# Retention decoder step: key-value product from rounded hi and lo parts, state updates beside the output projection, state transfers on GpSimd's queue

## The chip, the cores and the metric

The kernel runs on one core of one Trainium2 chip. Its time is the device time of one execution in microseconds (us); the number given for a kernel is the median of several runs. TensorE (PE) does the matmuls, VectorE (DVE) and ScalarE (ACT) do elementwise work, GpSimd (POOL) sets constants, and SyncE (SP) issues transfers. Each engine works through its own list in order and waits on semaphores for the others.

## The reference

One step of a hybrid decoder: a prompt of 528 rows (16 learned rows and 512 tokens) and 8 samples with one new row each, model width 1024. Layer 0 is a retention mixer and a gated FFN with a causal convolution of width 3; layer 1 is a short convolution mixer and a second such FFN; a last norm follows. The change is in the retention mixer, which has 4 heads with keys of 256 and values of 512:

```python
proj = rms_norm(x) @ w_in                      # q, k, v, gate
scores = (q @ k.T) * decay_mask
inner = scores @ v
kv = einsum('md,me->de', k * k_decay, v)       # the state that a chunk adds
s_new = exp(log_gamma * L) * s_prev + kv
o = group_norm(inner + (q @ s_prev) * cross_decay)
x = x + (silu(gate) * o) @ w_out
```

For the prompt, `s_prev` starts at zero. Each of the 8 samples has its own state of 256x512 per head, which is an input and, updated with that sample's one key and value row, an output. All is fp32.

## The kernel before

All weights come as 227 units of 128x1024 fp32 (512 KB). SyncE loads a unit into one of two raw slots (`RAW`); ScalarE rounds it (`split_hi`, L846, into `WH`), VectorE subtracts (`split_lo`, L1159, into `WL`). The rounded format is fp32r. A product of weights and activations is then three rounded matmuls, hi by hi, hi by lo and lo by hi (`three`, L405). There are four slots of split units; a split waits until TensorE has finished the unit four before it (`unit_done`), a load until the unit two before it is split.

The program runs four heads one after another, then FFN 0, the short convolution, FFN 1 and the final norm. A head has 16 units: 0 to 3 for queries and keys, 4 to 7 for values (L530, four blocks of 128 prompt rows in four PSUM banks), 8 to 11 for the gate, 12 to 15 for the output projection. Its stages on TensorE:

- queries and keys, which VectorE rotates (`rotate`);
- values; meanwhile ScalarE and VectorE fold the 8 sample states `S` with the samples' queries (`fold`, L917 and L1307), and TensorE takes the folds in (`samples`, L509);
- transposes of the keys (L546) and scores (L563), while ScalarE and VectorE copy the value rows `V` out of PSUM, two blocks each (L938; L1329 and L1331), and ScalarE copies the decayed key rows `KN` (L954);
- the key-value product (L573): plain fp32 matmuls of `KN` and `V`, 128x512, for two halves e of the key and blocks j = 0, 1 and then 2, 3; after blocks 0 and 1 ScalarE copies the middle state to `KM` (L970). Each half ends with a tail matmul (L579), already of rounded parts stacked in one operand;
- the inner product (L599 to L605), in plain fp32;
- the gate and the group norm, and then the output projection: units 12 to 15, two tiles of the output each, in PSUM slots that alternate. VectorE adds each pair to the residual (L1435, `x_written`). TensorE begins unit 14 when the additions of unit 12 are done and unit 15 when those of unit 13 are; the next head, or the FFN, begins its own first pair when those of unit 14 are done. In the last head each unit's additions are followed by norm tiles for the FFN (`norm_tile`: ScalarE rounds and squares, VectorE subtracts and sums); the FFN's statistic (L438) waits for all of the sums.

The update of sample state b is `outer` on ScalarE, two outer products of a broadcast value row `VB` by the sample's key into `G` (L948), and `update` on VectorE (L1351). Before, the eight updates of a head stand between the key-value product and the gate. `G` has two buffers of 1024 columns, so `outer(b)` waits for `update(b - 2)`.

SyncE's list mixes the weights with the head's decay constants `DEC`, the eight loads of `S` (L338), the value rows of the samples to a scratch in DRAM and back as a broadcast (L343, L347), the prompt's state (L351) and the eight stores of `S` (L354). A store waits for its update, the next head's load for the store.

Of the kernel before, what the change touches and what calls it, by code (L numbers as in the profile page):

```python
# [71 lines left out]
X_SETUP = 0  # L72
PAIR_A, PAIR_B = (1, 2), (0, 3)
# [24 lines left out]
def build(nc, io):  # L98
# [8 lines left out]
    with ctx:  # L107
# [31 lines left out]
        with ExitStack() as s2:  # L139
            with ExitStack() as s3:  # L140
                VB = sb("v_bcast", [P, NB, DV], scope=s3)
# [5 lines left out]
            V = sb("v_rows", [P, 5, DV], scope=s2)  # L147
            KN = sb("k_rows", [P, 4, DK], scope=s2)
            KT = sb("k_tail_stack", [P, DK], F32R, scope=s2)
            G = sb("gate", [P, 4 * N_RET], scope=s2)  # L150
            PR = sb("scores", [P, PCOL[4]], scope=s2)
            VS = sb("v_tail_stack", [P, DV], F32R, scope=s2)
# [72 lines left out]
        v_some = sem("v_some")  # L225
# [29 lines left out]
        def _(pool):  # L255
# [25 lines left out]

            pool.wait_ge(ys_out, 1)
# [4 lines left out]
        def _(sp):  # L287
# [19 lines left out]
            st_in = io["state_ret"][0].rearrange("b h (i e) v -> b h i (e v)", e=2)  # L307
            st_out = io["ret_s"][0].rearrange("b h (i e) v -> b h i (e v)", e=2)
            kv_dst = io["ret_p"][0, 0].rearrange("h (i e) v -> h i (e v)", e=2)

# [16 lines left out]
            def head(h, first):  # L327
                for n in range(4 if first else 0, 6):
# [6 lines left out]
                for b in range(NB):  # L335
                    if not first:
                        sp.wait_ge(s_out[b], 16 * h)
                    sp.dma_start(S[:, b, :], st_in[b, h]).then_inc(s_in[b], 16)  # L338
                for n in range(6, 11):
                    in_heads(h, n)  # L340

                sp.wait_ge(v_tail, 4 * h + 4)
                sp.dma_start(VSCR, V[16:24, 4, :]).then_inc(v_sent, 16)  # L343
                sp.wait_ge(v_sent, 16 * h + 16)
                for half in range(2):
                    b = half * NB // 2
                    sp.dma_start(VB[:, b:b + NB // 2, :], VSCR[b:b + NB // 2, :].partition_broadcast(P)).then_inc(vb_in[half], 16)  # L347
                for n in range(11, 14):
                    in_heads(h, n)
                sp.wait_ge(kv_ready, h + 1)  # L350
                sp.dma_start(kv_dst[h], KV).then_inc(kv_sent, 16)  # L351
                for b in range(NB):
                    sp.wait_ge(s_upd, NB * h + (b + 1))
                    sp.dma_start(st_out[b, h], S[:, b, :]).then_inc(s_out[b], 16)  # L354
                for n in range(14, 16):
                    in_heads(h, n)

            for h in range(HEADS):
                head(h, h == 0)
# [5 lines left out]
            def ffn_units(l):  # L365
                with sp.Fori(0, JF // 2) as i:
                    for n in range(4):
                        load(U_FFN_IN[l] + n, 4, i)
# [26 lines left out]
        def _(pe):  # L395
# [91 lines left out]
            def head(h, first, last):  # L487
# [53 lines left out]
                for j, (m0, mn) in enumerate(BLK):  # L541
                    for e in range(2):
                        at = (j % 2) * DK + e * P
                        if j == 4 and e == 0:
                            pe.wait_ge(v_some, 2 * h + 1)
# [5 lines left out]
                for j, (m0, mn) in enumerate(BLK):  # L551
                    if j == 0:
                        pe.wait_ge(v_ready, 3 * h + 2)
                        pe.wait_ge(v_some, 2 * h + 1)
                    elif j == 1:
                        pe.wait_ge(v_ready, 3 * h + 3)
                    elif j == 2:
                        pe.wait_ge(v_some, 2 * h + 2)
# [276 lines left out]
        def _(act):  # L835
# [73 lines left out]

            def head(h, first, last):  # L910
# [29 lines left out]
                def outer(b):  # L940

                    if b in (0, NB // 2):
                        act.wait_ge(vb_in[b // (NB // 2)], 16 * h + 16)
                    if b >= 2:
                        act.wait_ge(s_upd, 8 * h + (b - 1))
                    for e in range(2):
                        at = (b % 2) * 1024 + e * DV
                        fn(G[:, at:at + DV], VB[:, b, :], ACT.Copy, scale=KD8[:, e, b:b + 1]).then_inc(samp_kv, 1)  # L948

                act.wait_ge(dec_in, 16 * h + 16)  # L950
                act.wait_ge(knat_done, 2 * h + 1)
                for j in range(4):
                    src = PS[:, (6, 6, 7, 7)[j], (j % 2) * DK:(j % 2 + 1) * DK]
                    fn(KN[:, j, :], src, ACT.Copy, scale=DEC[:, DEC_ROW + j:DEC_ROW + j + 1]).then_inc(kn_ready, 1)  # L954
# [17 lines left out]
                if first:  # L972
                    act.wait_ge(prep_step, 12)
                outer(0)
                split_hi(7 + NS, U_HEAD, h)

                outer(1)
                for dt in range(4):
                    outer(dt + 2)
# [3 lines left out]
                outer(6)  # L983
                outer(7)
# [41 lines left out]
            for b in range(NB):  # L1026
                act.wait_ge(s_out[b], 16 * HEADS)

            def ffn(l, norm_no):
# [3 lines left out]
                def body(i, first):  # L1033
                    split_hi(u0 + NS, 4, i)
                    if first:
                        act.wait_ge(stat_done, norm_no + 1)
                        root(3, n_in // 2, halves(R[:, c0:]), rstd)
                    split_hi(u0 + 1 + NS, 4, i)
# [12 lines left out]
                    split_hi(u0 + 3 + NS, 4, i)  # L1051
                    for t in range(2):
# [99 lines left out]
        def _(dve):  # L1152
# [113 lines left out]

            def head(h, first, last):
# [56 lines left out]
                dve.wait_ge(v_ready, 3 * h + 1)  # L1324
# [3 lines left out]
                dve.wait_ge(v_acc, 3 * h + 2)  # L1328
                ts(V[:, 1, :], PS[:, 3, :], RN[:, 1:2], None, ALU.mult).then_inc(v_some, 1)  # L1329
                dve.wait_ge(unit_done, U_HEAD * h + (NS + 8))  # L1330
# [17 lines left out]
                def update(b):  # L1348
                    dve.wait_ge(samp_kv, 16 * h + (2 * b + 2))
                    at = (b % 2) * 1024  # L1350
                    stt(S[:, b, :], S[:, b, :], DEC[:, DEC_STATE:DEC_STATE + 1], G[:, at:at + 1024], ALU.mult, ALU.add).then_inc(s_upd, 1)  # L1351
# [5 lines left out]
                update(0)  # L1357
                split_lo(NS + 7, U_HEAD, h)
# [11 lines left out]
                for b in range(1, 5):  # L1370
                    update(b)
                for dt in range(1, 4):
                    channel_sum(dt)
                update(5)
# [9 lines left out]
                update(6)  # L1384
                update(7)
# [20 lines left out]
                dve.wait_ge(s_upd, NB * h + NB)  # L1406
# [24 lines left out]
                for p in range(4):  # L1431
# [15 lines left out]
            def ffn(l, norm_no):  # L1447
# [3 lines left out]
                def body(i, first):  # L1451
                    split_lo(u0 + NS, 4, i)
                    if first:
                        dve.wait_ge(rstd, norm_no + 1)
                        dve.reciprocal(R[:, c0:], R[:, c0:]).then_inc(r_ready, 1)
                        dve.wait_ge(r_ready, norm_no + 1)
                        if l == 1:
# [300 lines left out]
```

## Time and profile before

| | |
|---|---|
| median of 3 runs | 1457.04 us (1456.8 to 1457.08) |
| the profiled execution | 1458.02 us, span of its instructions 1454.7 us |
| TensorE busy | 1449.2 us |
| VectorE busy | 799.9 us |
| ScalarE busy | 543.2 us |
| granted TensorE clock | 1.000 (mean over the span) |
| HBM traffic | 118 GB/s on average |

A busy time is the time in which at least one instruction of the engine was in work. Matmuls overlap in the records, and their ends are modelled, so the distance between the starts of matmuls says more than the length of one.

### The profile page before, as it was taken

How to read it: one execution, taken by the hardware profiler on the slowest of the kernel's cores; microseconds unless marked ns; L12 is line 12 of the kernel's file. 1: busy time of each engine (PE TensorE's matmuls, PEld its weight loads, DVE VectorE, ACT ScalarE, POOL GpSimd, SP SyncE). 2: the span in 40 equal slices, each digit the busy share in tenths (PEclk: the TensorE clock that was granted, in tenths of full speed). 3: DMA queues.
4: the chain of work that ended last, by engine and by line, in shares of the span. 5: the costliest groups of instructions: out<-in, count | busy, mean ns of one | idle time of the engine just before them, and what ended most of it. 6: DMA issues, size and time to landing. Idle time of an engine off the chain costs nothing.

```text
span 1454.7 us, 27349 instructions
## 1 busy us (share of the span) xinstructions
PE 1449.2 (100%) x11428; PEld 1395.2 (96%) x11428; DVE 799.9 (55%) x1066; ACT 543.2 (37%) x776; POOL 2.9 (0%) x24
## 2 busy tenths in 40 slices
PE   9999999999999999999999999999999999999998
PEld 9699789879979999999999999999999999999998
DVE  7885577468458855555542427444565555553222
ACT  5552273264155543333331314222343333332222
POOL 0000000000000000000000000000000000000000
PEclk9999999999999999999999999999999999999999
DMA  8445253463444322222222222232223222222221
GB/s 302 149 186 192 96 225 107 180 232 104 166 162 178 115 89 87 89 98 87 87 93 100 87 88 88 88 97 92 89 89 100 87 87 99 88 87 101 92 88 59
DMA packets 47742, 171.94 MB, mean 118 GB/s; under 512 B 5608, under 2 KB 6248, under 8 KB 46624
## 3 DMA queue, kind: packets, MB, share of 16 engines
q1 hardware_dynamic: 47488, 170.76, 33.8%
q8 instruction: 62, 1.02, 0.3%
q14 instruction: 16, 0.13, 0.0%
q0 software_dynamic: 32, 0.03, 0.0%
q10 hardware_dynamic: 144, 0.00, 0.0%
HBM read 149.44 MB, written 21.55 MB: 118 GB/s over the span
## 4 chain that ended last, share of the span: by engine, by line
issue 100%; POOL 0%; POOLq 0%
POOLq L107 0%; POOL ident L266 0%; POOL h_tail L263 0%; POOL k_tail_stack L275 0%; POOL mean_v L259 0%; POOL ident L257 0%; POOL h_hi L261 0%; POOL h_lo L262 0%; POOL sample_ones L274 0%; POOL sample_ones L279 0%; POOL mean_d L258 0%; POOL late_q_decayed L276 0%; POOL seed L268 0%; POOL seed L269 0%; POOL seed L271 0%
## 5 line engine op out<-in xcount | busy, mean ns | idle before, releaser
L846 ACT ACTIVATE w_hi<-w_raw 128x1024 fp32r<-128x1024 f32 x227 | 240.1, 1059 | 671.4 <-PE ps L405 469.1
L405 PE MATMUL ps<-h_hi,w_hi 128*128 128x264 f32 (+2 forms) x2300 | 468.3, 285 | 0.4 <-DVE h_lo L1184 0.4
L405 PE MATMUL ps<-h_lo,w_hi 128*128 128x264 f32 (+2 forms) x2300 | 465.4, 284 | 0.0
L405 PE MATMUL ps<-h_hi,w_lo 128*128 128x264 f32 (+2 forms) x2300 | 464.9, 283 | 0.0
L1159 DVE TENSOR_TENSOR w_lo<-w_raw,w_hi 128x1024 fp32r<-128x1024 f32 x227 | 277.0, 1222 | 334.5 <-ACT w_hi L846 334.2
L405 PEld LDWEIGHTS ps<-h_hi,w_hi 128*128 128x128 f32 x2300 | 355.8, 188 | 1.5 <-issue 0.8
L405 PEld LDWEIGHTS ps<-h_hi,w_lo 128*128 128x128 f32 x2300 | 355.5, 188 | 0.0
L405 PEld LDWEIGHTS ps<-h_lo,w_hi 128*128 128x128 f32 x2300 | 355.3, 188 | 0.0
L695 PE MATMUL ps<-z_hi,w_lo 128*128 128x264 f32 (+1 forms) x704 | 144.7, 283 | 0.0
L695 PE MATMUL ps<-z_lo,w_hi 128*128 128x264 f32 (+1 forms) x704 | 144.6, 283 | 0.0
L695 PE MATMUL ps<-z_hi,w_hi 128*128 128x264 f32 (+1 forms) x704 | 144.6, 283 | 0.0
L695 PEld LDWEIGHTS ps<-z_hi,w_lo 128*128 128x128 f32 x704 | 110.1, 189 | 0.0
L695 PEld LDWEIGHTS ps<-z_lo,w_hi 128*128 128x128 f32 x704 | 109.9, 188 | 0.0
L695 PEld LDWEIGHTS ps<-z_hi,w_hi 128*128 128x128 f32 x704 | 109.8, 188 | 0.0
L1482 DVE TENSOR_TENSOR tmp<-ps,rms 128x524 f32<-128x524 f32 (+1 forms) x44 | 28.8, 696 | 76.1 <-PE ps L405 76.1
L1463 DVE TENSOR_TENSOR tmp<-ps,rms 128x528 f32<-128x528 f32 (+1 forms) x44 | 29.0, 701 | 67.9 <-PE ps L405 67.8
L530 PE MATMUL ps<-w_hi,h_hi 128*128 128x512 f32 x128 | 52.2, 408 | 0.0
L405 PE MATMUL ps<-ret_z_hi,w_lo 128*128 128x264 f32 x256 | 52.0, 285 | 0.0
L405 PE MATMUL ps<-ret_z_hi,w_hi 128*128 128x264 f32 x256 | 51.9, 284 | 0.0
L405 PE MATMUL ps<-ret_z_lo,w_hi 128*128 128x264 f32 x256 | 51.8, 284 | 0.0
L530 PE MATMUL ps<-w_hi,h_lo 128*128 128x512 f32 x128 | 50.5, 395 | 0.0
L530 PE MATMUL ps<-w_lo,h_hi 128*128 128x512 f32 x128 | 50.5, 394 | 0.0
(205 smaller groups left out, 1407.7 us busy)
## 6 DMA issues: line engine op xcount, KB each, us to landing
w_raw<-in_w_units_dram SPq DMA_DIRECT2D x227, 512.0 KB, 3.3
states<-in_state_ret_dram SPq DMA_DIRECT2D x32, 512.0 KB, 8.5
out_ret_s_dram<-states SPq DMA_DIRECT2D x32, 512.0 KB, 4.6
v_bcast<-v_scratch SPq DMA_DIRECT2D x8, 1024.0 KB, 5.6
x_res<-in_x_all_dram SPq DMA_DIRECT2D x8, 268.0 KB, 6.0
out_ret_p_dram<-tmp SPq DMA_DIRECT2D x4, 512.0 KB, 3.7
out_y_prompt_dram<-y_rows SPq DMA_DIRECT2D x4, 512.0 KB, 2.6
decay<-in_decay_dram SPq DMA_DIRECT2D x4, 299.5 KB, 3.8
```

Source lines behind the costliest of these rows:

```text
L405: out = mm(PS[:, 2 * s + half, at:at + n_col], a, b[:, lo:lo + n_col], start=first and n == 0, stop=last and n == 2)
L530: out = mm(PS[:, 2 + b, :], a, c, start=k == 0 and q == 0, stop=k == KD - 1 and q == 2)
L695: out = mm(PS[:, 2 * DOWN[t] + half, to:to + n_col], a, z[:, j, lo:lo + n_col], start=j == 0 and q == 0, stop=j == JF - 1 and q == 2)
L846: fn(WH[:, c % NS, :], RAW[:, c % NR, :], ACT.Copy).then_inc(hi_ready, 1)
L1159: tt(WL[:, c % NS, :], RAW[:, c % NR, :], WH[:, c % NS, :].bitcast(F32), ALU.subtract).then_inc(lo_ready, 1)
L1463: tt(halves(TMP[:, t, 0:n_in]), slot(PAIR_A[t], w), halves(R[:, c0:]), ALU.mult).then_inc(up_read, 1)
L1482: tt(halves(TMP[:, t, 4:n_in]), slot(PAIR_B[t], n_out // 2), halves(R[:, c0 + 4:]), ALU.mult).then_inc(gate_read, 1)
```

## The change

- The key-value product is made of rounded parts. ScalarE writes all four blocks of `V` (plain fp32, still used by the inner product) and, with a second pass over PSUM, their rounded form `VH`; VectorE subtracts to get `VL`. ScalarE's key copy gives `KNH`, VectorE's `k_rest` the remainder `KNL`. TensorE does three rounded matmuls where it did one in fp32, and waits for `VL` and `KNL`. ScalarE's copies to `KM` move ahead of the split of unit 9.
- The updates move to the output projection. `UPDATES` says which go with which unit: in heads 0 to 2 states 0 and 1 with unit 13, 2 and 3 with unit 14, 4 to 7 with unit 15; in the last head 0 and 1 with unit 12, 2 and 3 with unit 13, and 4 to 7 in the first iteration of FFN 0. On ScalarE they stand after the unit's split and ahead of the norm tiles, on VectorE after both.
- GpSimd issues the loads and stores of the states, the scratch, the broadcasts and the prompt's state. SyncE keeps the weights and the decay.
- Buffers: `VH` and `VL` lie where `VB` lay, `VB` over `V`, `PR` and `VS`, `G` over `KNH` and `KNL`.

```diff
+UPDATES = (((), (0, 1), (2, 3), (4, 5, 6, 7)), ((0, 1), (2, 3), (), ()))
...
# GpSimd
+            def state_stream(h):
+                def broadcast():
+                    for half in range(2):
+                        b = half * NB // 2
+                        pool.dma_start(VB[:, b:b + NB // 2, :], VSCR[b:b + NB // 2, :].partition_broadcast(P)).then_inc(vb_in[half], 16)
+                for b in range(NB):
+                    if h > 0:
+                        pool.wait_ge(s_out[b], 16 * h)
+                    elif b == 0:
+                        pool.wait_ge(ss_sum, 7)
+                    pool.dma_start(S[:, b, :], st_in[b, h]).then_inc(s_in[b], 16)
+                pool.wait_ge(v_tail, 4 * h + 4)
+                pool.dma_start(VSCR, V[16:24, 4, :]).then_inc(v_sent, 16)
+                pool.wait_ge(kv_ready, h + 1)
+                pool.dma_start(kv_dst[h], KV).then_inc(kv_sent, 16)
+                pool.wait_ge(v_sent, 16 * h + 16)
+                pool.wait_ge(inner_done, 4 * h + 4)
+                broadcast()
+                for b in range(NB):
+                    pool.wait_ge(s_upd, NB * h + (b + 1))
+                    pool.dma_start(st_out[b, h], S[:, b, :]).then_inc(s_out[b], 16)
...
# SyncE, in head(h): DEC waits for the last update of the head before, then
+                for n in range(6, 16):
                     in_heads(h, n)
+                for n in range(4):
+                    next_unit(h, n)
...
# TensorE
-                pe.wait_ge(kn_ready, 4 * h + 4)
                 for js in ((0, 1), (2, 3, 4)):
                     for e in range(2):
                         if js[0] == 2:
                             pe.wait_ge(mid_ready, 2 * h + e + 1)
+                        else:
+                            pe.wait_ge(kn_lo, 4 * h + 2 * e + 2)
+                            pe.wait_ge(v_lo, 4 * h + 4)
                         for j in js[:2]:
-                            out = mm(PS[:, 6 + e, :], KN[:, j, e * P:(e + 1) * P], V[:, j, :], start=j in (0, 2), stop=j == 1)
+                            kh, kl = KNH[:, j, e * P:(e + 1) * P], KNL[:, j, e * P:(e + 1) * P]
+                            for q, (k, v) in enumerate(((kh, VH), (kh, VL), (kl, VH))):
+                                out = mm(PS[:, 6 + e, :], k, v[:, j, :], start=j in (0, 2) and q == 0, stop=j == 1 and q == 2)
...
# ScalarE
-                for b in (0, 2):
-                    act.wait_ge(v_acc, 3 * h + b + 1)
+                for b in range(4):
+                    if b < 3:
+                        act.wait_ge(v_acc, 3 * h + b + 1)
+                    else:
+                        act.wait_ge(unit_done, U_HEAD * h + (NS + 8))
                     fn(V[:, b, :], PS[:, 2 + b, :], ACT.Copy, scale=RN[:, b:b + 1]).then_inc(v_ready, 1)
+                    fn(VH[:, b, :], PS[:, 2 + b, :], ACT.Copy, scale=RN[:, b:b + 1]).then_inc(v_hi, 1)
...
-                split_hi(5 + NS, U_HEAD, h)
                 for e in range(2):
                     act.wait_ge(mid_done, 2 * h + e + 1)
                     fn(KM[:, e * DV:(e + 1) * DV], PS[:, 6 + e, :], ACT.Copy).then_inc(mid_ready, 1)
+                split_hi(5 + NS, U_HEAD, h)
...
                     if not (last and p == 3):
                         split_hi(12 + p + NS, U_HEAD, h)
+                    for b in UPDATES[last][p]:
+                        outer(h, b)
                     if last:
                         for k in (2 * p, 2 * p + 1):
...
# VectorE
-                ts(V[:, 1, :], PS[:, 3, :], RN[:, 1:2], None, ALU.mult).then_inc(v_some, 1)
-                ts(V[:, 3, :], PS[:, 5, :], RN[:, 3:4], None, ALU.mult).then_inc(v_some, 1)
+                for b in range(4):
+                    dve.wait_ge(v_ready, 5 * h + b + 2)
+                    dve.wait_ge(v_hi, 4 * h + b + 1)
+                    tt(VL[:, b, :], V[:, b, :], VH[:, b, :].bitcast(F32), ALU.subtract).then_inc(v_lo, 1)
+                def k_rest(j):
+                    if j % 2 == 0:
+                        dve.wait_ge(kn_ready, 4 * h + j + 2)
+                    src = PS[:, 6 + j // 2, (j % 2) * DK:(j % 2 + 1) * DK]
+                    stt(KNL[:, j, :], src, DEC[:, DEC_ROW + j:DEC_ROW + j + 1], KNH[:, j, :].bitcast(F32),
+                        ALU.mult, ALU.subtract).then_inc(kn_lo, 1)
+                k_rest(0)
+                k_rest(1)
...
+                k_rest(2)
+                k_rest(3)
...
                     if last:
                         for k in (2 * p, 2 * p + 1):
                             norm_tile(k, 1, C_RET, N_RET, D_FFN)
+                    for b in UPDATES[last][p]:
+                        update(h, b)
...
# ScalarE and VectorE, first iteration of FFN 0, after the root and its reciprocal
+                        for b in range(4, NB):
+                            outer(HEADS - 1, b)
...
+                            for b in range(4, NB):
+                                update(HEADS - 1, b)
```

## Rows read from the trace of the kernel before

**Rows 1.** The page, busy time and share of each engine.
```profile
PE 1449.2 (100%) x11428; PEld 1395.2 (96%) x11428; DVE 799.9 (55%) x1066; ACT 543.2 (37%) x776; POOL 2.9 (0%) x24
```

**Rows 2.** The waits: who waited for whom, us in total, times, longest.
```profile
ACT w_hi L846 <- PE ps L405: 469.1, 139, 4.8
...
PE ps L452 <- POOL mean_d L258: 1.1, 1, 1.1
```

**Rows 3.** The timeline of TensorE around head 1's product: start, length, operation.
```profile
179.94 0.39 PE L530 MATMUL ps<-w_lo,h_hi 128*128 128x512 f32 x1
...
180.64 0.39 PE L530 MATMUL ps<-w_lo,h_hi 128*128 128x512 f32 x1
...
184.96 5.42 PE L573 MATMUL ps<-v_rows,k_rows 128*128 128x512 f32 x12
...
192.40 0.80 PE L599 MATMUL ps<-scores,v_rows 128*128 128x248 f32 x4
```

**Rows 4.** The same view in head 0, after an fp32 stretch.
```profile
36.96 0.50 PE L530 MATMUL ps<-w_hi,h_hi 128*128 128x512 f32 x1
...
37.30 0.39 PE L530 MATMUL ps<-w_hi,h_lo 128*128 128x512 f32 x1
```

**Rows 5.** The timeline of ScalarE and VectorE around head 1's product.
```profile
179.67 0.69 ACT L938 ACTIVATE v_rows<-ps,rms_rows 128x512 f32<-128x512 f32 x1 [2.10 <-PE ps L530]
...
182.00 1.57 ACT L954 ACTIVATE k_rows<-ps,decay 128x256 f32<-128x256 f32 x4 [1.64 <-PE ps L546]
...
187.17 0.58 ACT L970 ACTIVATE tmp<-ps 128x512 f32<-128x512 f32 x1
...
185.29 0.16 DVE L1340 TENSOR_TENSOR scores_end<-ps,decay 24x24 f32<-24x24 f32 x1
...
185.48 0.47 DVE L1342 SCALAR_TENSOR_TENSOR k_tail_stack<-ps,decay,k_tail_stack 16x256 fp32r<-16x256 f32 x1
```

**Rows 6.** Windows: head 2's output projection, head 3's first two weight stages.
```profile
227.14:250.50 23.36, 23.36 (x195) 23.36 (x194) 15.02 (x20) 7.65 (x9) 0.00 (x0) 1.00 0.35 114
...
250.50:274.00 23.50, 23.50 (x194) 23.50 (x193) 8.69 (x11) 3.18 (x3) 0.00 (x0) 1.00 0.56 215
```

**Rows 7.** The second unit of the last head's output projection, as a window.
```profile
479.30:485.13 5.83, 5.83 (x51) 5.83 (x49) 5.83 (x8) 5.11 (x8) 0.00 (x0) 1.00 0.33 112
```

**Rows 8.** The timeline of VectorE in the last head.
```profile
454.25 2.47 DVE L1351 SCALAR_TENSOR_TENSOR states<-states,decay,gate 128x1024 f32<-128x1024 f32 x2
...
476.58 1.32 DVE L1435 TENSOR_TENSOR x_res<-x_res,ps 128x528 f32<-128x528 f32 x2 [0.86 <-PE ps L405]
...
482.43 1.31 DVE L1435 TENSOR_TENSOR x_res<-x_res,ps 128x528 f32<-128x528 f32 x2
...
487.51 1.31 DVE L1435 TENSOR_TENSOR x_res<-x_res,ps 128x528 f32<-128x528 f32 x2
...
492.60 1.31 DVE L1435 TENSOR_TENSOR x_res<-x_res,ps 128x528 f32<-128x528 f32 x2
...
496.20 0.71 DVE L1172 TENSOR_TENSOR tmp<-tmp 128x528 f32<-128x528 f32 x1
```

**Rows 9.** The timeline of ScalarE in the last head.
```profile
433.77 2.54 ACT L948 ACTIVATE gate<-v_bcast,dec_k 128x512 f32<-128x512 f32 x4
...
478.17 1.06 ACT L846 ACTIVATE w_hi<-w_raw 128x1024 fp32r<-128x1024 f32 x1 [3.89 <-DMA w_raw<-in_w_units_dram]
```

**Rows 10.** The timeline of TensorE: fourth unit, FFN's first matmul, the FFN's statistic.
```profile
485.13 0.41 PE L405 MATMUL ps<-ret_z_hi,w_hi 128*128 128x264 f32 x2
...
490.96 0.41 PE L405 MATMUL ps<-h_hi,w_hi 128*128 128x264 f32 x2
...
498.29 1.05 PE L438 MATMUL ps<-tmp,mean_d 128*128 128x264 f32 x4
```

**Rows 11.** A window of five microseconds while head 2's states are loaded.
```profile
260.00:265.00 5.00, 5.00 (x43) 5.00 (x42) 1.54 (x2) 1.06 (x1) 0.00 (x0) 1.00 1.03 409
```

**Rows 12.** The timeline of ScalarE, second fold of head 2.
```profile
287.98 2.57 ACT L917 ACTIVATE tmp<-states,dec_q 128x512 f32<-128x512 f32 x4 [2.45 <-PE ps L509]
```

More of the change, by code:

```diff
@@ L146, in build @@
             Q, K = O[:, 0:2, :], O[:, 2:4, :]
-            V = sb("v_rows", [P, 5, DV], scope=s2)
-            KN = sb("k_rows", [P, 4, DK], scope=s2)
+            with ExitStack() as s6:
+                V = sb("v_rows", [P, 5, DV], scope=s6)
+                PR = sb("scores", [P, PCOL[4]], scope=s6)
+                VS = sb("v_tail_stack", [P, DV], F32R, scope=s6)
+            VB = sb("v_bcast", [P, NB, DV], scope=s2)
             KT = sb("k_tail_stack", [P, DK], F32R, scope=s2)
+            with ExitStack() as s7:
+                KNH = sb("k_rows_hi", [P, 4, DK], F32R, scope=s7)
+                KNL = sb("k_rows_lo", [P, 4, DK], F32R, scope=s7)
             G = sb("gate", [P, 4 * N_RET], scope=s2)
-            PR = sb("scores", [P, PCOL[4]], scope=s2)
-            VS = sb("v_tail_stack", [P, DV], F32R, scope=s2)
             SE = sb("scores_end", [P, 24], scope=s2)
@@ L279, in _ @@
                 pool.memset(ONE_OF[:, g, 24 + 4 * g:26 + 4 * g], 1.0).then_inc(const_ready, 1)
+            st_in = io["state_ret"][0].rearrange("b h (i e) v -> b h i (e v)", e=2)
+            st_out = io["ret_s"][0].rearrange("b h (i e) v -> b h i (e v)", e=2)
+            kv_dst = io["ret_p"][0, 0].rearrange("h (i e) v -> h i (e v)", e=2)
+            def state_stream(h):
[19 more added lines that the diff above has]
+                    pool.dma_start(st_out[b, h], S[:, b, :]).then_inc(s_out[b], 16)
+            for h in range(HEADS):
+                state_stream(h)
             pool.wait_ge(ys_out, 1)
@@ L325, in _, with ffn_in_unit, next_unit, head @@
             sp.dma_start(CF[:], io["ffn_consts"]).then_inc(ffn_in, 16)
-            def head(h, first):
-                for n in range(4 if first else 0, 6):
+            def ffn_in_unit(l, i, n):
+                load(U_FFN_IN[l] + 4 * i + n)
+            def next_unit(h, n):
+                if h < HEADS - 1:
+                    in_heads(h + 1, n)
+                else:
+                    ffn_in_unit(0, 0, n)
+            def head(h, first, last):
+                for n in range(4, 6):
                     in_heads(h, n)
@@ L334, in head @@
                 sp.dma_start(DEC[:], io["decay"][h]).then_inc(dec_in, 16)
[L335 to L339, printed above, removed]
-                    in_heads(h, n)
[L342 to L356, printed above, removed]
+                for n in range(6, 16):
+                    in_heads(h, n)
+                for n in range(4):
+                    next_unit(h, n)
             for h in range(HEADS):
-                head(h, h == 0)
+                head(h, h == 0, h == HEADS - 1)
             for l in range(2):
@@ L365, in ffn_units @@
             def ffn_units(l):
-                with sp.Fori(0, JF // 2) as i:
+                if l == 1:
+                    for n in range(4):
+                        ffn_in_unit(l, 0, n)
+                for n in range(4):
+                    ffn_in_unit(l, 1, n)
+                with sp.Fori(2, JF // 2) as i:
                     for n in range(4):
@@ L908, in _, with outer @@
             fn(RN[:], PS[:, 3, 300:305], ACT.Sqrt, bias=EPST[:]).then_inc(rows_rstd, 2)
+            def outer(h, b):
+                if b == 0:
+                    act.wait_ge(z_mul, 8 * h + 8)
+                if b in (0, NB // 2):
+                    act.wait_ge(vb_in[b // (NB // 2)], 16 * h + 16)
+                if b >= 2:
+                    act.wait_ge(s_upd, 8 * h + (b - 1))
+                for e in range(2):
+                    at = (b % 2) * 1024 + e * DV
+                    fn(G[:, at:at + DV], VB[:, b, :], ACT.Copy, scale=KD8[:, e, b:b + 1]).then_inc(samp_kv, 1)
             def head(h, first, last):
@@ L935, in head @@
                 fn(VT, PS[:, 0, 0:P], ACT.Copy, scale=RN[:, 4:5]).then_inc(v_ready, 1)
-                for b in (0, 2):
-                    act.wait_ge(v_acc, 3 * h + b + 1)
-                    fn(V[:, b, :], PS[:, 2 + b, :], ACT.Copy, scale=RN[:, b:b + 1]).then_inc(v_ready, 1)
[L940 to L948, printed above, removed]
+                for b in range(4):
+                    if b < 3:
+                        act.wait_ge(v_acc, 3 * h + b + 1)
+                    else:
+                        act.wait_ge(unit_done, U_HEAD * h + (NS + 8))
+                    fn(V[:, b, :], PS[:, 2 + b, :], ACT.Copy, scale=RN[:, b:b + 1]).then_inc(v_ready, 1)
+                    fn(VH[:, b, :], PS[:, 2 + b, :], ACT.Copy, scale=RN[:, b:b + 1]).then_inc(v_hi, 1)
                 act.wait_ge(dec_in, 16 * h + 16)
+                if first:
+                    act.wait_ge(prep_step, 12)
                 act.wait_ge(knat_done, 2 * h + 1)
@@ L1037, in body @@
                         root(3, n_in // 2, halves(R[:, c0:]), rstd)
+                    if first and l == 0:
+                        for b in range(4, NB):
+                            outer(HEADS - 1, b)
                     split_hi(u0 + 1 + NS, 4, i)
@@ L1051, in body @@
                     split_hi(u0 + 3 + NS, 4, i)
+                    if first and l == 0:
+                        for b in range(NB):
+                            act.wait_ge(s_out[b], 16 * HEADS)
                     for t in range(2):
@@ L1369, in head @@
                 tt(KV, PS[:, 6:8, :].rearrange("p e v -> p (e v)"), KM, ALU.add).then_inc(kv_ready, 1)
-                for b in range(1, 5):
-                    update(b)
+                split_lo(NS + 7, U_HEAD, h)
                 for dt in range(1, 4):
                     channel_sum(dt)
-                update(5)
                 dve.wait_ge(gstat_done, 2 * h + 1)
```

48 lines of the change are left out of this document (13 added, 35 removed).

## The prediction

> **What bounds the kernel now.** I read the page first: TensorE is busy for 1449.2 of 1454.7 us, VectorE for 55%, ScalarE for 37% [rows 1]. Matmul records overlap, so a busy TensorE could still hide waits; the table of waits settles it. ScalarE waits longest for TensorE, 469.1 us, and the only entry of TensorE in the longest sixty is 1.1 us at the start [rows 2]. TensorE's order of work sets the end: fewer matmul microseconds come straight off the time, and any wait put into its order is added in full. The profiled execution took 1458.02 us by the clock of the runs, 3.3 us of it outside the span, and lies 1.0 us above the median of 1457.04; I work out differences and take them from the median.
>
> **The key-value product.** For head 1, the PE timeline puts the old product, its two tail matmuls (L579) included, from 184.96 to 192.40: 7.44 us [rows 3]. Afterwards it is 24 rounded matmuls of 128x512 and the same two tails, 26 of one shape. That shape stands in the V projection (L530): starts at 179.94 and 180.64 are three steps apart, 0.233 us each [rows 3]. 26 x 0.233 = 6.06 us. The product now begins with a change from fp32 to rounded operands; where L530 follows fp32 work its first step is 0.34 instead of 0.23 us [rows 4], so I add 0.1 for it and 0.1 for the change back: 6.26 us. Saved: 1.18 us a head, 4.7 us in four. With changes of format at nothing it would be 1.38, or 5.5.
>
> The Trainium skill ("FP8 and Floating Point Precision", TensorE Precision Notes) says that true fp32 takes four passes through the array. Three rounded passes for four would take a quarter off the 16 records of L573 and save about 1.7 us a head, 6.9 us in all, and the sum would end at 1454.4 by it. The row speaks for less: a rounded pass with its own weights is 0.233 us here, and I keep that.
>
> **What must be ready for it.** ScalarE now copies four V blocks twice, where it copied two once. A pair takes 1.2 us (0.69 for one, L938, overlapping by 0.1 [rows 5]) and a block comes every 1.4 us, six matmuls of 0.233, so only the last pair follows the last matmul: 181.1 to 182.4. The K copies (four in 1.57, begun at 182.00 [rows 5]) slide by 0.3. VectorE loses its two V copies and gains four subtractions of 128x512 and four K remainders; I price a remainder like the smaller one of L1342, 0.47 [rows 5], and a subtraction at 0.7, like the 128x528 operation at 496.20 [rows 8]. The last subtraction ends at 183.1 and the first two remainders at 184.0, 0.9 before TensorE asks at 184.96. Remainders 2 and 3 push the score work back: its last operation (L1340), at 185.29 now, comes at about 186.0. ScalarE rounds the scores, then copies the first half of the middle state (L970, 0.58 [rows 5]): ready at 187.3, wanted at 184.96 + 0.1 + 12 x 0.233 = 187.85. The spare 0.5 us is the thinnest here. So no wait is counted; if that chain is 0.9 late, 0.4 a head comes back and the saving is 3.1. Queued behind it on ScalarE is only the unit 9 split, put behind the copies and wanted some 10 us later.
>
> **State updates, heads 0 to 2.** Eight updates cost VectorE 1.2 us each (two in 2.47 [rows 8]) and ScalarE the same (four outer products in 2.54 [rows 9]), 10 us on either. In the output projection VectorE is busy for 15.02 of 23.36 us and in the next head's first two weight stages for 8.69 of 23.50; ScalarE 7.65 and 3.18 [rows 6]. Additions to x come before updates in program order, updates 4 to 7 run some 8 us into the next head (additions 1.3, split 1.2, updates 5), and the split they delay is of a unit wanted 23 us after that head begins. I cost them at nothing; the cover is this idle time and the three units split ahead, and without it the price is up to 10 us a head. The inner stage that they leave gets shorter on VectorE, which frees no TensorE time, as TensorE did not wait there.
>
> **State updates, last head.** Here the cover is gone. In the second unit (479.30 to 485.13) VectorE is busy all 5.83 us already [rows 7], with norm tiles. Now 0 and 1, then 2 and 3, go behind the norm tiles of the first two units.
> - First unit. ScalarE's split began at 478.17, after 3.89 us of waiting for weights [rows 9], the norm tiles followed it, and VectorE reached the next additions at 482.43 [rows 8]. Updates 6 and 7 at 454.25 disappear from the chain that lets those weights load, about 1.7 of their 2.47 us (the rest becomes waiting for the root of the statistic), so the split can start at 476.5, when TensorE finishes the unit: 1.6 earlier. ScalarE's four outer products then stand before the norm tiles (+2.5), and two updates before the additions (+2.4): 482.43 - 1.6 + 2.5 + 2.4 = 485.7. The second addition ends at 487.0; TensorE needs it for its fourth unit at 485.13 [rows 10]. Wait: 1.9.
> - Second unit. Additions to additions took 487.51 - 482.43 = 5.08 [rows 8]; two updates make it 7.5: 493.2, done at 494.5. The FFN's first matmul wanted them at 490.96 [rows 10]: 3.5 late in all.
> - Third unit on. 5.09 to the additions at 492.60 and 4.3 more to the end of the last sum of squares at 496.9 [rows 8] gives 502.6. The statistic stood at 498.29 [rows 10], now 501.8: 0.8 more.
>
> Loss: 4.3 us, once. Next comes the root, which TensorE asks for three tiles later, 3 x 1.46 us (a quarter of 5.83 [rows 7]); one split, the table load and the root on ScalarE just fit into that. Then updates 4 to 7 before VectorE's first read of the FFN, needed a 23 us iteration later: absorbed. Bounds: if ScalarE's outer products cost the chain nothing the same steps give 1.0 + 0.8 = 1.8; if the weights come no earlier, 5.9.
>
> **Transfers.** Per head GpSimd issues eight state loads, eight stores, the V scratch row, two broadcasts and the prompt state, each behind its own wait in one queue; SyncE keeps weights and decay. TensorE waited for none of them. Weights gain nothing, since no wait of TensorE ends with them. The broadcasts start after the inner product and have about 25 us until the first outer product. Loads of the next head start at 8 us into it instead of 3.6; the old ones moved up to 409 GB/s [rows 11], and even at half that 4 MB are in by 28 us, while the second fold reads from 37.5 us on (287.98 [rows 12], in a head that begins at 250.5 [rows 6]). Nothing counted.
>
> **Sum.** -4.7 + 4.3 = -0.4: 1456.6 us. The bounds give -5.5 + 1.8 to -3.1 + 5.9, so 1453.3 to 1459.8.
>
> **Rivals.**
> - The last head absorbs its updates: 1457.0 - 4.7 = 1452.3. For it: VectorE and ScalarE stood idle before the first unit's end and waited for weights there. Against: VectorE's full unit [rows 7].
> - Loads by GpSimd are slow. Eight loads from 258.4 must be in by 290, 3.9 us each; beyond that each of heads 1 to 3 waits. At 5 us each the last is 8.5 late, 25 in three heads: at most 1482. For it: no large transfer from GpSimd is in this trace. Against: the rate of [rows 11] is three times what is needed.
> - The saving is eaten: the chain to the middle state comes 1.7 us late in every head and the shorter product only waits. 1457.0 + 4.3 = 1461.3. It decides from 0.5 us of lateness on; the spare times above speak against it.
>
> The Trainium skill ("SBUF — State Buffer", Who interferes with whom) warns that GpSimd can't write descriptors while VectorE runs a copy in a two-port mode. That is the second rival's mechanism; VectorE's long work near the loads is additions, products and subtractions, so the trace gives it little ground.
>
> **Chances.** Forecast 0.62, absorbed 0.18, slow loads 0.10, eaten 0.10. What a measurement can tell is about 0.2%, 2.9 us: below 1454.1 counts as faster, above 1460.0 as slower. The forecast's low bounds add 0.07 to the 0.18 of absorbed; its high ones add nothing much to the 0.20 of the last two. So 0.25, 0.55, 0.20. The range, 1452.2 to 1460.5, reaches the absorbed case and leaves out the two slower ones, 0.2.
>
> **What would show it.** Right: in each head the product takes about 6.3 us with no wait of TensorE; in the last head TensorE waits for the additions of L1435 before its fourth unit (about 1.9), before the FFN (1.6) and before the statistic (0.8). Wrong: a wait of TensorE on the remainders or on L970's copies, on the folds of heads 1 to 3, or no wait at L1435; product steps other than 0.233; a lower granted clock behind the new waits.

## The result and the profile after

The changed kernel takes 1460.39 us (median of 12 runs, 1460.09 to 1460.66), the kernel before beside it on the same chip 1457.00 (12 runs). The ratio is 1.0022, 95% interval 1.0014 to 1.0030: slower by 3.4 us, where I had forecast 0.4 us faster. The time lies inside the forecast range, 0.1 us below its upper end; the direction does not lie with the forecast.

I read the same views as before the change, and then the one that I had not read. First the timeline of TensorE around head 1's product, to be read beside [rows 3]:

```profile
183.66 0.50 PE L601 MATMUL ps<-v_rows_hi,k_rows_hi 128*128 128x512 f32 x1
183.99 0.39 PE L601 MATMUL ps<-v_rows_lo,k_rows_hi 128*128 128x512 f32 x1
184.22 0.39 PE L601 MATMUL ps<-v_rows_hi,k_rows_lo 128*128 128x512 f32 x1
...
189.58 0.40 PE L607 MATMUL ps<-v_tail_stack,k_tail_stack 96*128 96x512 f32 x1
189.81 0.58 PE L627 MATMUL ps<-scores,v_rows 128*128 128x248 f32 x2
```

From start to start the product takes 189.81 - 183.66 = 6.15 us where it took 7.44. Only the first step is longer than 0.23 us (183.66 to 183.99, 0.33); the change back to fp32 at the end (189.58 to 189.81) costs nothing. That is 1.29 us a head, 5.2 in four.

Then all of TensorE's waits (in total, times, longest):

```profile
PE ps L434 <- DVE x_res L1474: 1.9, 1, 1.9
PE ps L434 <- DVE h_lo L1218: 1.4, 3, 0.8
PE ps L481 <- POOL mean_d L264: 1.1, 1, 1.1
PE ps L467 <- DVE tmp L1206: 0.5, 1, 0.5
```

No wait on the remainders, the middle state or the folds is among them. The first is the one forecast for the last head (L1474 is the old L1435). The second and third stand in the first 14 us of the program. They cost the changed kernel nothing against before: in both kernels TensorE goes on from the last of these waits at the same time, 13.66 us after and 13.67 before. The timeline of TensorE there answers to [rows 10]:

```profile
481.98 0.48 PE L434 MATMUL ps<-ret_z_hi,w_hi 128*128 128x264 f32 x2 [1.85 <-DVE x_res L1474]
482.30 0.50 PE L434 MATMUL ps<-ret_z_lo,w_hi 128*128 128x264 f32 x2
482.60 0.65 PE L434 MATMUL ps<-ret_z_hi,w_lo 128*128 128x264 f32 x2
483.04 0.65 PE L434 MATMUL ps<-ret_z_hi,w_hi 128*128 128x264 f32 x2
...
489.41 0.47 PE L434 MATMUL ps<-h_hi,w_hi 128*128 128x264 f32 x2
...
497.44 1.16 PE L467 MATMUL ps<-tmp,mean_d 128*128 128x264 f32 x4 [0.48 <-DVE tmp L1206]
```

Without the 1.85 us wait the fourth unit would have begun at 480.13, 5.0 us ahead of before (485.13). It began 3.15 ahead; the FFN began 1.55 ahead (489.41 against 490.96) and the statistic 0.85 ahead (497.44 against 498.29). So the last head gave back 5.0 - 0.85 = 4.15 us, in three portions of 1.85, 1.60 and 0.70. The second portion has a form that I did not expect. In these windows of the changed kernel the granted clock, as a share of full speed, stands ahead of the last two columns:

```profile
482.60:485.70 3.10, 3.10 (x16) 0.50 0.81 282
485.70:489.40 3.70, 3.70 (x31) 0.98 0.51 195
```

Behind its wait TensorE ran 3.1 us at 1.2 GHz, so the unit took 7.43 us, not 5.83. The additions that the FFN needs were ready no earlier, as the timeline of VectorE shows, to be read beside [rows 8]:

```profile
478.13 2.47 DVE L1304 SCALAR_TENSOR_TENSOR states<-states,decay,gate 128x1024 f32<-128x1024 f32 x2
480.53 1.31 DVE L1474 TENSOR_TENSOR x_res<-x_res,ps 128x528 f32<-128x528 f32 x2
...
485.61 2.47 DVE L1304 SCALAR_TENSOR_TENSOR states<-states,decay,gate 128x1024 f32<-128x1024 f32 x2
488.00 1.31 DVE L1474 TENSOR_TENSOR x_res<-x_res,ps 128x528 f32<-128x528 f32 x2
...
496.68 0.71 DVE L1206 TENSOR_TENSOR tmp<-tmp 128x528 f32<-128x528 f32 x1
```

They end at 489.31, and TensorE goes on at 489.41. At full clock it would have waited there instead; the fall of the clock took the place of that wait and added nothing to it. Two later runs, which meet the same first wait without a fall of the clock, bear this out (under "The last head's updates").

So far the changed kernel is ahead by 0.85 us, and it stays ahead: VectorE's last useful operation starts at 1450.62 (L1692) where it started at 1451.37 (L1648). First before, then after:

```profile
1451.37 0.23 DVE L1648 TENSOR_TENSOR y_samples<-y_t,rms 128x64 f32<-128x64 f32 x1
...
1450.62 0.23 DVE L1692 TENSOR_TENSOR y_samples<-y_t,rms 128x64 f32<-128x64 f32 x1
```

The 3.4 us are lost behind it. All engines close on the program's last line, L107 before and L108 after. Each engine closes its list there with an instruction called DRAIN. In that line's instructions the numbers between the slashes are the length in ns (shortest, median, longest), and the two behind the comma are the starts, first and last, in us. Before:

```profile
L107 DVEq DRAIN  x1: 264/264/264, 1451.4 to 1451.4; - x1
L107 POOLq DRAIN  x1: 2437/2437/2437, 1451.9 to 1451.9; - x1
L107 SPq DRAIN  x1: 7/7/7, 1454.5 to 1454.5; - x1
L107 POOLq EVENT_SEMAPHORE  x2: 17/17/17, 1454.5 to 1454.6; - x2
```

After:

```profile
L108 DVEq DRAIN  x1: 266/266/266, 1450.6 to 1450.6; - x1
L108 POOLq DRAIN  x1: 7254/7254/7254, 1451.1 to 1451.1; - x1
L108 SPq DRAIN  x1: 7/7/7, 1453.7 to 1453.7; - x1
L108 POOLq EVENT_SEMAPHORE  x2: 17/17/17, 1458.4 to 1458.5; - x2
```

Before, GpSimd's DRAIN ended at 1451.9 + 2.4 = 1454.3, just ahead of SyncE's last wait (1454.5). After, SyncE was done at 1453.7, and the program stood 4.7 us for a DRAIN of 7.25 us. What GpSimd did differently stands on the page, in the table of queues (packets, MB, share). The first row is that of before, the second that of after:

```profile
q0 software_dynamic: 32, 0.03, 0.0%
...
q0 software_dynamic: 11104, 44.14, 7.7%
```

GpSimd issued 81 transfers instead of one, and its closing DRAIN is three times as long. Whether one is the cause of the other, and what the length goes with, is for the runs.

The page of the kernel before held a hint: its chain that ended last ended with GpSimd's queue, on this line, and led back into GpSimd's idle time:

```profile
issue 100%; POOL 0%; POOLq 0%
```

I had passed over it, because a chain made of "issue" alone seemed to say nothing.

### The profile page after: what moved, and what is told of

Same layout as the page of the kernel before. It is cut to its first block, busy times and chain, and to the rows that moved or that the text cites. A ratio compares the mean times of both kernels' runs of the same rounds, so it can differ in the third digit from the quotient of the medians.

```text
span 1458.6 us, 27424 instructions
## 1 busy us (share of the span) xinstructions
PE 1445.2 (99%) x11460; PEld 1401.7 (96%) x11460; DVE 809.8 (56%) x1090; ACT 557.4 (38%) x800; POOL 45.1 (3%) x104
## 4 chain that ended last, share of the span: by engine, by line
issue 65%; PE 31%; DVE 2%; ACT 1%; DMA 0%; SPq 0%; POOLq 0%; POOL 0%; ACTq 0%; DVEq 0%
PE ps L434 18%; PE ps L559 6%; PE ps L601 2%; PE ps L630 1%; PE ps L587 1%; PE ps L627 1%; PE ps L632 1%; DVE states L1304 1%; PE ps L530 1%; PE ps L467 1%; PE ps L538 1%; DMA w_raw<-in_w_units_dram 0%; PE ps L575 0%; ACT gate L948 0%; DVE rms L1496 0%
```

## The experiments

The runs were timed in three groups, each on one chip with the kernel before beside them; it read 1456.82, 1456.91 and 1456.88 us. The changed kernel was timed only beside the result, so differences from its 1460.39 us go from one group to another; the kernel before differs by 0.2 us between all of them.

**The last transfer moved away from GpSimd.**

```diff
 # GpSimd
-            pool.wait_ge(ys_out, 1)
-            pool.dma_start(io["y_sample"], ...).then_inc(ys_sent, 16)
 # SyncE, behind the rows of y_prompt
+            sp.wait_ge(ys_out, 1)
+            sp.dma_start(io["y_sample"], ...).then_inc(ys_sent, 16)
```

> The changed kernel, with one transfer moved: the last one of GpSimd, y_sample, is issued by SyncE behind its last weight load, so that GpSimd's program ends with the last state store near 510 us and its closing DRAIN (7.25 us after the change, 2.44 us before) runs there, beside a whole millisecond of other work. Theory 1 (the 3.4 us lost are GpSimd's closing DRAIN, which grew with the 80 transfers it issues): the end comes with SyncE's last transfer, which landed at 1453.7 us in the changed kernel against a program end near 1458.5, so 4.5 to 4.8 us less: 1455.7 us, 0.999 of the kernel before. Theory 2 (the loss is elsewhere in the useful work, or SyncE's own closing instructions take the place of the DRAIN): no change, 1460.4 us. Theory 3 (the DRAIN stays at the end whoever issues last, since all engines close together): GpSimd's DRAIN row still near 1451 us and 7 us long, 1460 us.

Measured: 1455.73 us, ratio to before 0.9992 (95% interval 0.9983 to 1.0001, as in the brackets below). The closing line, from the same view:

```profile
L108 POOLq DRAIN  x1: 7162/7162/7162, 509.3 to 509.3; - x1
...
L108 SPq DRAIN  x1: 7/7/7, 1453.5 to 1453.5; - x1
```

The DRAIN is nearly as long as in the changed kernel, with 80 transfers for 81, but it runs at 509.3 us beside other work. The time falls by 4.7 us. Theory 1 holds; theories 2 and 3 fall.

**A drain in the middle.** Here GpSimd keeps every transfer.

```diff
+            pool.drain()
             pool.wait_ge(ys_out, 1)
             pool.dma_start(io["y_sample"], ...).then_inc(ys_sent, 16)
```

> The changed kernel, with one instruction more: GpSimd drains once between its last state store (near 510 us) and the wait for y_sample, which it still issues at the end. No transfer moves. Theory 1a (the closing DRAIN pays for all software transfers issued since the last drain): the middle drain takes that and the closing one falls back to about 2.4 us, 1455.6 us. Theory 1b (the closing DRAIN's length goes with the whole queue's history, whatever was drained earlier): the closing row stays at 7.2 us, 1460.4 us. Theory 2 (the loss is elsewhere): 1460.4 us and no link with the DRAIN rows.

Measured: 1455.80 us, 0.9993 (0.9984 to 1.0002). The added instruction's line and the closing one:

```profile
L319 POOLq DRAIN  x1: 7166/7166/7166, 509.6 to 509.6; - x1
...
L108 POOLq DRAIN  x1: 2455/2455/2455, 1451.2 to 1451.2; - x1
```

The middle drain takes 7.17 us for the 80 transfers ahead of it, and the closing one is back at the length of before. A DRAIN of GpSimd pays for what was issued since the one ahead of it (1a), and paying early costs nothing here.

**The same edit on the kernel before**, as a control.

> The kernel before, with y_sample issued by SyncE at the end instead of GpSimd; nothing else is changed. Its closing DRAIN of 2.44 us ended at 1454.3 us, just ahead of SyncE's last wait (1454.5 us), so taking it from the end should give nothing: 1456.8 us, and the 4.7 us that the same edit gave on the changed kernel are then what the 80 transfers brought. Rival (the edit gains for a reason of its own, such as an earlier landing of y_sample): about 1452 us here too.

Measured: 1456.74 us beside 1456.88 for before, 0.9998 (0.9989 to 1.0007). The edit has no gain of its own. With no transfer at all on its queue GpSimd's DRAIN is short:

```profile
L107 POOLq DRAIN  x1: 386/386/386, 2.5 to 2.5; - x1
```

**What the length goes with.** Three runs vary the number of transfers, their bytes and their issuer. The first adds 80 small ones to the kernel before:

```diff
+            for n in range(80):
+                pool.dma_start(TINY[n], IDENT[:, 0:16]).then_inc(tiny, 16)
+            pool.wait_ge(tiny, 16 * 80)
```

> The kernel before, with 80 transfers more on GpSimd's queue, all near the start of the program, from a constant tile to a scratch buffer: 128 rows of 64 bytes each, 0.66 MB in all, so nearly the number of transfers and of rows that the change put there and 1.5% of its bytes. SyncE keeps all state transfers, and the computation is that of before. If the closing DRAIN goes with the number of transfers or of their rows: its row grows from 2.44 to 7.2 us, ends near 1459.1 instead of 1454.3, and the time is 1456.8 + 4.6 = 1461.4 us. If it goes with the bytes, or with how lately the transfers were issued: 2.4 us and 1456.8.

Measured: 1461.88 us, 1.0034 (1.0022 to 1.0047). Its closing line:

```profile
L107 POOLq DRAIN  x1: 7252/7252/7252, 1452.6 to 1452.6; - x1
```

And its queue, on the page:

```profile
q0 software_dynamic: 2592, 0.69, 0.2%
```

The same length as the changed kernel's 7.254, with a sixty-fourth of the bytes and a quarter of the packets, and with its small transfers at the start of the program, where GpSimd also waits for them to land, 1.4 ms ahead: neither bytes nor packets nor lateness set it. This run slows the kernel before by 5.0 us, about what the DRAIN costs the changed kernel, with nothing of the change but the number of transfers.

The second splits the stores of the changed kernel:

```diff
-                    pool.dma_start(st_out[b, h], S[:, b, :]).then_inc(s_out[b], 16)
+                    for at in (0, 64):
+                        pool.dma_start(st_out[b, h][at:at + 64], S[at:at + 64, b, :]).then_inc(s_out[b], 16)
```

> The changed kernel, with each of the 32 state stores issued as two transfers of 64 partitions: 113 transfers on GpSimd's queue where the changed kernel has 81, the same bytes and the same number of rows. If the closing DRAIN goes with the number of transfers, at (7.25 - 2.44) / 80 = 0.060 us each: 7.25 + 32 x 0.060 = 9.2 us, time 1462.3 us. If it goes with rows or bytes: 7.25 us, 1460.4 us.

Measured: 1462.98 us, 1.0042 (1.0028 to 1.0055), 2.6 above the changed kernel; the DRAIN is longer by 2.65:

```profile
L108 POOLq DRAIN  x1: 9906/9906/9906, 1451.5 to 1451.5; - x1
```

The bytes are the same and so are the rows, so the number of transfers decides. (Each transfer also signals its completion once, so the two counts can't be told apart here.) I had expected 9.2 from a straight line through 1 and 81 transfers; the step from 81 to 113 is steeper, 0.083 us each.

The third gives the loads back to SyncE:

```diff
 # GpSimd, in state_stream(h): the loop over the loads goes
 # SyncE, behind DEC
+                for b in range(NB):
+                    if h > 0:
+                        sp.wait_ge(s_out[b], 16 * h)
+                    sp.dma_start(S[:, b, :], st_in[b, h]).then_inc(s_in[b], 16)
```

> The changed kernel, with the 32 state loads issued by SyncE again, behind the decay factors as in the kernel before; GpSimd keeps 49 of its 81 transfers. Were the DRAIN 0.060 us for each transfer: 2.44 + 48 x 0.060 = 5.3 us, time 1460.4 - 1.9 = 1458.5 us. Rival, from the queues: SyncE's weight loads of the next head stand again behind its waits for the state stores; if that costs TensorE anything, the time is above 1458.5, and a wait of TensorE or ScalarE on a weight unit shows early in heads 1 to 3.

Measured: 1457.69 us, 1.0006 (0.9997 to 1.0015), 2.7 less than the changed kernel, for a DRAIN 2.6 shorter:

```profile
L108 POOLq DRAIN  x1: 4641/4641/4641, 1450.9 to 1450.9; - x1
```

SyncE's weights behind those waits cost nothing, so the rival falls, and again the straight line through 1 and 81 was wrong (5.3 expected). Two runs with fewer small transfers fill in the lower end.

> The kernel before, with 20 small transfers more on GpSimd's queue near the start, 21 in all; only the length of the closing DRAIN is read. So far: 1 transfer 2.44 us, 49 transfers 4.64, 80 transfers 7.16, 81 transfers 7.25, 113 transfers 9.91, so 0.082 us a transfer from 49 on, a line that meets 2.44 us at 22 transfers. If the DRAIN has a floor of 2.44 us and that line beyond it: 2.44 us here. If it bends slowly from the first transfer on: between 2.9 and 3.4 us.

> As with 20 small transfers, now 40, 41 in all. Floor and line: 4.64 - 8 x 0.082 = 3.98 us. Slow bend (a chord from 2.44 us at 1 transfer to 4.64 at 49): 4.27 us.

Measured, in one execution each, for 21 and for 41 transfers:

```profile
L107 POOLq DRAIN  x1: 3649/3649/3649, 1452.4 to 1452.4; - x1
...
L107 POOLq DRAIN  x1: 3984/3984/3984, 1451.9 to 1451.9; - x1
```

| transfers on GpSimd's queue since its last drain | its DRAIN, us |
|---|---|
| 0 | 0.39 |
| 1 | 2.44 |
| 21 | 3.65 |
| 41 | 3.98 |
| 49 | 4.64 |
| 80 | 7.16 and 7.17 |
| 81 | 7.25 and 7.25 |
| 113 | 9.91 |

From 41 on the lengths lie on one line of (9.91 - 3.98) / 72 = 0.082 us a transfer, within 0.03. Below it neither shape that I offered holds: 41 transfers lie on the line, 21 lie above both. What the DRAIN does in that time no view shows, so the shape of the lower end stays open.

**The last head's updates.** This run takes them off the second and third additions of the last projection; heads 0 to 2 stay.

```diff
-UPDATES = (..., ((0, 1), (2, 3), (), ()))
+UPDATES = (..., ((), (), (), ()))
...
 # ScalarE, ahead of the units of the output projection; VectorE with update
+                if last:
+                    outer(h, 0)
+                    outer(h, 1)
...
 # both, first iteration of FFN 0
-                        for b in range(4, NB):
+                        for b in range(2, NB):
```

> The changed kernel, with the last head's state updates spread otherwise: updates 0 and 1 are put ahead of that head's first output-projection unit, where VectorE and ScalarE have nothing to do, and 2 to 7 into the first iteration of the FFN, where the kernel before has 0 to 7; the other heads are not touched. Theory 1 (my forecast's term: the four updates inside the last projection cost 4.3 us at TensorE): the 1.9 us wait of TensorE on x_res ahead of the fourth unit and the half clock behind it go, 3.5 to 4.3 us less: 1456.1 to 1456.9 us. Rival (the 4.3 us are only moved into the FFN, where two updates fewer than before don't help and the same DVE chain is late): no change, 1460.4 us.

Measured: 1455.93 us, 0.9991 (0.9982 to 1.0000), 4.5 less than the changed kernel and so a little more than the 3.5 to 4.3 expected. Its list of TensorE's waits is down to two lines:

```profile
PE ps L434 <- DVE h_lo L1221: 1.3, 3, 0.7
PE ps L481 <- POOL mean_d L264: 1.1, 1, 1.1
```

And the window from 484 to 486 us, half clock in the changed kernel, is whole:

```profile
484.00:486.00 2.00, 2.00 (x19) 1.00 0.73 244
```

The wait on x_res, the half clock and the wait of the statistic are all gone, and the DRAIN is unchanged (7.26 us). Six updates in the FFN's first iteration cost nothing that can be seen: the rival falls. (The expectation puts the eight updates of the kernel before there too; they are not, its last ones start at 454.25 [rows 8].)

What the half clock was worth, two other runs tell. The stores in halves leave the last head as the change made it. Their timeline of TensorE, and two windows with the granted clock:

```profile
482.29 0.49 PE L435 MATMUL ps<-ret_z_hi,w_hi 128*128 128x264 f32 x2 [1.86 <-DVE x_res L1475]
...
489.68 0.51 PE L435 MATMUL ps<-h_hi,w_hi 128*128 128x264 f32 x2 [1.29 <-DVE x_res L1475]
```

```profile
482.00:484.00 2.00, 1.71 (x14) 1.00 0.89 225
484.00:486.00 2.00, 2.00 (x19) 1.00 0.92 264
```

The first wait is as long as in the changed kernel, but the clock stays at 2.4 GHz, and TensorE waits a second time, ahead of the FFN. From the fourth unit to the FFN it takes 7.39 us, against 7.43 with the half clock. The run with the plain product, below, shows the same: waits of 1.86 and 1.29, full clock, 7.39 us (487.11 to 494.50). So VectorE's additions set this time, the half clock added nothing to speak of, and the 1.85 us wait alone does not decide whether the clock falls.

**The product of before in the changed kernel.**

```diff
-                            for q, (k, v) in enumerate(((kh, VH), (kh, VL), (kl, VH))):
-                                out = mm(PS[:, 6 + e, :], k, v[:, j, :], ...)
+                            out = mm(PS[:, 6 + e, :], KNH[:, j, e * P:(e + 1) * P], V[:, j, :], start=j in (0, 2), stop=j == 1)
```

with `KNH` in plain fp32 and without `VH`, `VL`, `KNL` and the work that makes them.

> The changed kernel, with the key-value product of before (one fp32 product of normalized keys and values, no hi and lo parts and none of their work on ScalarE and VectorE); transfers and updates stay as changed. If the product saved what the critical chain shows (7.44 to 6.25 us for each of four heads, and a head period of 118.96 for 120.25 us): + 4.8 to + 5.2, 1465.2 to 1465.6 us. If the shorter product is given back elsewhere in the head: less, down to 1460.4 us.

Measured: 1465.85 us, 1.0063 (1.0049 to 1.0076), 5.5 above the changed kernel. The timeline of TensorE in head 1:

```profile
184.92 5.42 PE L598 MATMUL ps<-v_rows,k_rows_hi 128*128 128x512 f32 x12
...
192.37 0.69 PE L624 MATMUL ps<-scores,v_rows 128*128 128x248 f32 x3
```

It takes 7.45 us again, 1.30 more than 6.15. Nothing of the shorter product is given back in the heads.

**Both places mended.** The edits of the first and of the last but one run together.

> The changed kernel with both edits: y_sample issued by SyncE at the end, and the last head's updates 0 and 1 ahead of its output projection with 2 to 7 in the FFN's first iteration. If both theories hold and the two places add: 1460.4 - 4.7 - 4.0 = 1451.7 us, 0.9963 of the kernel before. If only the DRAIN theory holds: 1455.7. If neither: 1460.4.

Measured: 1451.21 us, 0.9961 (0.9947 to 0.9974), 5.6 less than before. The places add: from here the DRAIN alone costs 1455.93 - 1451.21 = 4.7 us and the last head alone 1455.73 - 1451.21 = 4.5, and both together 9.2 (1460.39 - 1451.21). This version beats both kernels.

## Why the prediction was wrong

**The step that failed** is the paragraph on transfers, which ends with "Nothing counted". It priced the moved transfers by what waits for their data: queues, landing times, folds. That part was right in the changed kernel's trace: no wait of TensorE ends with one of them, and the loads land in 8.9 us by the median where they landed in 8.5. What it left out is that GpSimd must close its own list, and that its DRAIN grows with the transfers it issues: 4.8 us more for 80. SyncE, which had issued them before, paid nothing of the kind: its DRAIN takes 7 ns in both kernels, with 336 transfers issued before and 256 after. I had counted each transfer's queue and waits, but not what remains to be done at the end of the issuing engine's list, and so not that a transfer far ahead of the end can lengthen the end. It could be seen beforehand that GpSimd's DRAIN, 2.4 us for one transfer, ended only 0.2 us ahead of SyncE's last wait, without any spare time. How it grows could not be seen. That the time still lies inside the forecast range is luck: the range was made of the terms that were priced, and this one was not among them.

The Trainium skill ("VectorE: DVE Perf Modes", The DRAIN you can't avoid) says that the DRAINs of preamble and postamble are about 12 ns on every engine, always the same. Whether it means those on the program's last line no run shows. SyncE's 7 ns there would fit; VectorE's 264 ns before and 266 after do not, and GpSimd's least of all, with 0.39 to 9.91 us by its number of transfers. For the last line the measurement decides.

**The key-value product:** right in kind, small in size. Forecast 6.26 us and 1.18 saved, measured 6.15 and 1.29. The matmuls take the 0.233 us that the V projection showed; of the two changes of format that I priced at 0.1 each, only the one into rounded operands costs (0.33 for the first step instead of 0.23). No operand is late: the table of waits has none at L601. The rule of the Trainium skill that I weighed against the row ("FP8 and Floating Point Precision", TensorE Precision Notes: four passes for fp32) would have given about 1.7 us a head; the row was nearer.

**State updates, heads 0 to 2:** nothing counted, and no wait of TensorE is found there; with both other places mended the kernel is 5.6 us faster than before, all that the product gives and a little more.

**State updates, last head:** forecast 1.9, 1.6 and 0.8, measured 1.85, 1.60 and 0.70; 4.3 and 4.15 in all. The steps behind it were of mixed quality: the additions came at 480.53 and 488.00, some 5 us ahead of the 485.7 and 493.2 that I worked out on the clock of before, as the whole head had moved ahead by the shorter products; the differences are what hold. The middle portion came as half a clock and not as a wait. A lower granted clock behind the new waits was on the prediction's list of signs that it is wrong, but it added nothing: where the clock stayed full, the forecast wait ahead of the FFN was there, and the same time was lost (7.39 us against 7.43).

**The rivals:** "absorbed" falls, as the last head's loss is there and goes with its updates. "Slow loads by GpSimd" falls by the landing times. "The saving is eaten" gave 1461.3, near the measured time, but by a mechanism that is not there: the product keeps its whole saving (5.5 us by the run that undoes it). The Trainium skill's warning on GpSimd's descriptors beside VectorE ("SBUF — State Buffer", Who interferes with whom) finds no sign here: the loads land in 8.9 us by the median where they took 8.5.

**The sum with measured terms:** -5.2 (product) + 4.15 (last head) = -1.0 at the end of the useful work (0.75 by VectorE's last operation), then 4.8 for the DRAIN: +3.8 to +4.1 in the profiled spans, which differ by 1458.6 - 1454.7 = 3.9, and 3.4 in the medians; where the 0.5 between the two lies no view shows.

## What to carry to other kernels

An engine that takes over transfers can get a closing cost that the other never had, as GpSimd did here: look at the last line of each engine's list, at who closes last and by how much, before you call a transfer free. If GpSimd issues many, let its list end early, with the last output given to another engine, or drain it once in a stretch where it has nothing to do; either gave back 4.7 us here. And place moved elementwise work by the slack ahead of the next engine's need: two updates ahead of the projection and six in the FFN were free, four inside the projection cost 4.2 us by the trace and 4.5 by the medians.

## What the runs showed of the hardware

GpSimd's DRAIN grows with the number of transfers that it issued since its last drain, and with neither their bytes nor their age: 2.44 us for one, 7.25 for 81 of 44 MB and 7.25 for 81 of 0.7 MB, 0.082 us for each from 41 to 113. SyncE's closing DRAIN took 7 ns, with 336 transfers issued before and 256 after. Behind a wait of 1.85 us TensorE ran 3.1 us at 1.2 GHz in the changed kernel; behind the same wait of 1.86 us in two other runs its clock stayed at 2.4, and what decides between the two no run shows. The first rounded matmul behind fp32 ones took a step of 0.33 us instead of 0.23; the step from the last rounded one to fp32 was not longer.
